# A bidirectional mLSTM and gated feed-forward block on eight cores: contiguous weight layouts, a split last group, and a second gate buffer, other engine and other banks in the last backward sweep

## What is computed

```
h = modulate(rmsnorm(x, norm1_g), sh1, sc1)
z = h @ w_in                       # q,k | v | o | u,v of the gating unit | merge gates | 16 gate columns
qk = silu(centred_conv(qk, conv_w, conv_b))
hA = mlstm_bidirectional(qh, kh, vh, gates)        # forward scan + flipped backward scan, 4 heads x 256
y_a = rmsnorm_per_head(hA) * mh_g * sigmoid(o_a)
y_b = gelu(u_b) * (w_s applied to layernorm(gelu(v_b)) in chunks of 128 + b_s)
x = x + g1 * ((sigmoid(mg_a) * y_a + sigmoid(mg_b) * y_b) @ w_out)
h2 = modulate(rmsnorm(x, norm2_g), sh2, sc2)
x = x + g2 * (square(relu(h2 @ w1)) @ w2)
out = rmsnorm(x, normf_g)
```

## Time and profile before

| | us |
|---|---|
| median of 3 runs | 2370.88 |
| lowest, highest | 2370.76, 2378.68 |
| profiled execution | 2383.2 |
| span of its slowest core (core 1) | 2381.6 |
| span of its fastest core (core 2) | 2346.8 |

### The profile page before, as it was taken

The page is one execution under the profiler, slowest core; times in us unless marked ns, Lnnn a source line. Parts: engine busy times, 40 slices in busy tenths (PEclk is TensorE's granted clock), DMA queues, the critical chain, the costliest instruction groups (busy, mean ns, idle before and its releaser), DMA issues.

```text
span 2381.6 us, 49251 instructions; the slowest of 8 cores (2346.8 to 2381.6 us)
## 1 busy us (share of the span) xinstructions
PE 2219.5 (93%) x15036; PEld 1339.7 (56%) x15036; DVE 1403.2 (59%) x3065; ACT 1129.8 (47%) x2274; POOL 948.9 (40%) x1154
## 2 busy tenths in 40 slices
PE   5989999979899999999867999999999999999997
PEld 1444545446566555555523566666666666666664
DVE  2757787768788878878758733343333334333432
ACT  4644554378676666666535533333333333333332
POOL 1646666112377666656646612212222222212221
PEclk7999999999999999999979999999999999999998
DMA  9645454225866755645666620111111111111000
GB/s 303 175 92 143 124 139 125 76 37 81 84 82 84 133 96 96 146 87 100 113 158 189 201 84 30 48 54 54 54 50 50 54 54 54 54 54 54 30 17 36
DMA packets 141937, 219.96 MB, mean 92 GB/s; under 512 B 15655, under 2 KB 96103, under 8 KB 136686
## 3 DMA queue, kind: packets, MB, share of 16 engines
q1 hardware_dynamic: 104718, 187.16, 25.2%
q0 software_dynamic: 36960, 29.66, 13.4%
HBM read 196.08 MB, written 79.71 MB: 116 GB/s over the span
## 4 chain that ended last, share of the span: by engine, by line
PE 75%; DVE 8%; DMA 7%; issue 6%; POOL 2%; ACT 1%; DVEq 0%; SPq 0%; POOLq 0%; ACTq 0%
PE ps L359 73%; DVE arena L399 5%; PE ps L371 2%; DMA hf_d<-arena 2%; POOL arena L394 1%; ACT arena L379 1%; DMA arena<-w_vum 1%; DVE arena L394 1%; DMA mixa_d<-arena 1%; DMA arena<-x 1%; DMA mix_d<-arena 1%; DMA arena<-wg_d 1%; DMA arena<-hf_d 1%; DMA w_d<-w 0%; DVE arena L391 0%
## 5 line engine op out<-in xcount | busy, mean ns | idle before, releaser
L359 PE MATMUL ps<-arena 128*128 128x512 bf16 (+7 forms) x14012 | 2176.9, 321 | 129.5 <-DVE arena L399 46.9
L359 PEld LDWEIGHTS ps<-arena 128*128 128x128 bf16 (+1 forms) x14012 | 1279.3, 98 | 986.7 <-issue 227.8
L394 POOL TENSOR_TENSOR arena<-arena 128x1 f32<-128x1 f32 (+3 forms) x648 | 697.5, 1084 | 1057.6 <-ACT arena L379 352.9
L399 DVE SCALAR_TENSOR_TENSOR arena<-ps,arena 128x256 bf16<-128x256 f32 (+6 forms) x1474 | 606.1, 414 | 635.0 <-ACT arena L379 489.4
L379 ACT ACTIVATE arena<-ps 128x256 f32<-128x256 f32 (+2 forms) x972 | 496.7, 524 | 848.5 <-PE ps L359 719.3
L379 ACT ACTIVATE arena<-arena 128x514 bf16<-128x514 f32 (+5 forms) x558 | 403.7, 733 | 266.0 <-DVE arena L399 98.3
L399 DVE SCALAR_TENSOR_TENSOR arena<-arena 128x256 bf16<-128x256 f32 (+3 forms) x257 | 271.6, 1057 | 63.8 <-POOL arena L394 24.4
L379 ACT ACTIVATE arena<-ps,arena 128x512 f32<-128x512 f32 (+3 forms) x512 | 252.9, 519 | 117.2 <-DVE arena L1049 31.6
L394 DVE TENSOR_TENSOR arena<-ps,arena 128x512 bf16<-128x512 f32 (+4 forms) x294 | 169.2, 583 | 104.4 <-PE ps L359 102.2
L391 POOL TENSOR_SCALAR arena<-arena 128x1 f32<-128x1 f32 (+2 forms) x317 | 152.1, 482 | 149.4 <-ACT arena L379 121.2
L399 DVE SCALAR_TENSOR_TENSOR arena<-arena,ps 128x514 f32<-128x514 f32 x240 | 178.7, 745 | 28.4 <-PE ps L359 25.0
(11 more groups left out here) (17 smaller groups left out, 86.8 us busy)
## 6 DMA issues: line engine op xcount, KB each, us to landing
arena<-x SPq DMA_DIRECT2D x64, 512.0 KB, 4.6
arena<-w_ada SPq DMA_DIRECT2D x8, 2048.0 KB, 10.2
hf_d<-arena SPq DMA_DIRECT2D x128, 128.0 KB, 4.1
arena<-hf_d SPq DMA_DIRECT2D x128, 128.0 KB, 3.3
w_d<-w POOLq DMA_DIRECT2D x32, 512.0 KB, 8.6
out<-arena SPq DMA_DIRECT2D x32, 512.0 KB, 3.2
arena<-w_d SPq DMA_DIRECT2D x13, 1024.0 KB, 5.9
arena<-w_vum SPq DMA_DIRECT2D x12, 1024.0 KB, 16.9
```

The lines of the kernel that those rows point to most:

```text
L359: ins = e.matmul(o_, l_, r_, start=st, stop=sp)
L394: return E(eng, lambda e, o_=o_, a_=a_, b_=b_, op=op: e.tensor_tensor(o_, a_, b_, op), reads, writes, 0.6 if op == ALU.pow else vcost(eng, ...
L399: e.scalar_tensor_tensor(o_, a_, sc, b_, op0, op1), reads, writes, vcost("dve", o_))
```

## The change

1. The host packs w_qkv, w_og, w_out, w1 and w2 so that each casting transfer reads one contiguous run and writes one; the number and bytes of the transfers stay.
2. In the head x tiles 2 and 3 are asked for after w_vum piece 3.
3. Of the extra buffers, gv[2] moves to the second half of wad[5], and vn[2..4] all lie in wad[7].
4. For head 3 the gate weights have a buffer of their own (wog2, at base_b, where wqkv was), loaded once the last block is prepared (nxt == 31) instead of at hF = 4; wog is then free for feed-forward weights.
5. In the last sweep the sigmoid's scaling is an activation Copy on ACT instead of an operation on DVE, and the backward numerator alternates between banks 4 and 5.
6. In the last group the last three ffn2 steps are done for the first 128 rows and then for the second, each followed by final_last: as final, but in halves of 512 columns, straight from the banks, with DVE doing the second half's sums.

```diff
@@ head and stage 2
-            if n in (1, 3, 4):
-                load_x({1: 2, 3: 3, 4: 4}[n])
+            if n == 3:
+                load_x(2)
+                load_x(3)
+            if n == 4:
+                load_x(4)
...
-                dst, c0, rr = wq_d[h][j][:, 2 * m:2 * m + 2, :], (0, 1024, 2048)[j] + h * 256, R("wq_d", h, j, m)
+                ps_ = slice(32 * m, 32 * m + 32)
+                dst, src, rr = wq_d[h][j][ps_].rearrange("p a b -> p (a b)"), w_qkv[h][j][ps_], R("wq_d", h, j, m)
...
-            DMA("pool", dst, w_in[m * 256:(m + 1) * 256, c0:c0 + 256].rearrange("(kc p) n -> p kc n", p=128), [], [rr], gs_, pace=after)
+            DMA("pool", dst, src, [], [rr], gs_, pace=after)
...
-        SCH.alias([("wad", 7)], [("gv", 2, 0), ("gv", 2, 1), ("vn", 2), ("vn", 3)])
+        SCH.alias([("wad", 7)], [("vn", 2), ("vn", 3), ("vn", 4)])
...
-        gv.append(xbuf[1][:, 0, :])
-        vx = xbuf[1][:, 1, :].bitcast(BF16)
-        vn += [vx[:, 0:1024], vx[:, 1024:2048], wad[5][:, 1024:1536].bitcast(BF16)]
+        gv.append(wad[5][:, 1024:2048])
+        vx = wad[7].bitcast(BF16)
+        vn += [vx[:, j * 1024:(j + 1) * 1024] for j in range(3)]
...
-        SCH.alias([("gu", 2, 0), ("gu", 2, 1), ("gu", 3, 0), ("gu", 3, 1), ("gv", 2, 0), ("gv", 2, 1), ("vn", 2), ("vn", 3)], [("wst",)])
+        SCH.alias([("gu", 2, 0), ("gu", 2, 1), ("gu", 3, 0), ("gu", 3, 1), ("vn", 2), ("vn", 3), ("vn", 4)], [("wst",)])
@@ mLSTM
+        def RW(h):
+            return R("wog2") if h == 3 else R("wog")
+
         def load_og(h):
-            DMA("sp", wog, wg_d[h], [R("wg_d", h, j, m) for j in range(2) for m in range(4)], [R("wog")], wog_sem)
+            if h == 3:
+                wogs.append(alloc([128, 8, 512], BF16, ["wog2"], at=base_b))
+            DMA("sp", wogs[h // 3], wg_d[h], [R("wg_d", h, j, m) for j in range(2) for m in range(4)], [RW(h)], wog_sem[h // 3])
...
+        def BNB(h, i):
+            return (4, 5)[i % 2] if h == 3 else 5
...
-                TS("dve" if hF is None else "pool", tg[k2], tg[k2], 0.5, 0.5, ALU.mult, ALU.add, [RT], [RT])
+                if hF is None:
+                    ACTF(tg[k2], tg[k2], AF.Copy, [RT], [RT], scale=0.5, bias=0.5)
+                else:
+                    TS("pool", tg[k2], tg[k2], 0.5, 0.5, ALU.mult, ALU.add, [RT], [RT])
...
-                casts.append((w1_d[j][:, 4 * m:4 * m + 4], w1[m * 512:(m + 1) * 512, j * 512:(j + 1) * 512].rearrange("(kc p) n -> p kc n", p=128), R("w1_d", j, m)))
+                casts.append((w1_d[j][64 * m:64 * m + 64].rearrange("p a b -> p (a b)"), w1[j][64 * m:64 * m + 64], R("w1_d", j, m)))
...
-            if 1 < hF:
+            if 1 < hF < 4:
                 load_og(hF - 1)
...
+                if nxt == 31:
+                    load_og(3)
@@ feed-forward
+        def final_last(g, s_):
...
+            for hh, cs in enumerate(hv):
+                TT("dve", tf[s_][:, cs], banks[4 + 2 * s_ + hh][:, :], g2s[:, cs], ALU.mult, [PB(4 + 2 * s_ + hh), R("g2s")], [R("tf", s_, hh)])
+                TT("dve" if s_ else "pool", X[:, cs], tf[s_][:, cs], X[:, cs], ALU.add, [R("tf", s_, hh), R("xg", kg, s_)], [R("xl", s_, hh)])
+                ACTF(tf[s_][:, cs], X[:, cs], AF.Square, [R("xl", s_, hh)], [R("tf", s_, hh), R("s5", so, hh)],
+                     accum_out=sm4[:, so + 3 + hh:so + 4 + hh])
...
+            for hh, cs in enumerate(hv):
+                STT(tf[s_][:, cs], X[:, cs], sm4[:, so + 5:so + 6], nfs[:, cs], ALU.mult, ALU.mult,
+                    [R("xl", s_, hh), R("r5", so), R("nfs")], [R("tf", s_, hh)])
+                out_ops.append(DMA("sp", out[i * 128:(i + 1) * 128, cs], tf[s_][:, cs], [R("tf", s_, hh)], [R("out", i, hh)], (ob_sem, mxi_sem)[hh][s_]))
...
-                ffn2(g, ft)
+                if nx is not None or ft < 29:
+                    ffn2(g, ft)
+                elif ft == 31:
+                    for s_ in range(2):
+                        for f_ in (29, 30, 31):
+                            ffn2(g, f_, (s_,))
+                        final_last(g, s_)
```

More of the change, by code:

```diff
@@ L262, in build_program @@
     w_gt = din("w_gt", [128, 128])
+    w_qkv = din("w_qkv", [4, 3, 128, 2048])
+    w_og = din("w_og", [4, 128, 4096])
     bifb = din("bifb", [128, 512])
@@ L845, in build_program @@
         sml = alloc([128, NSM * 8], F32, [(nm, m) for nm in ("sml", "sq") for m in range(NSM)])
-        wog = alloc([128, 8, 512], BF16, ["wog"])
-        wog_sem = new_dsem()
+        wogs = [alloc([128, 8, 512], BF16, ["wog"])]
+        wog_sem = [new_dsem() for _ in range(2)]
         for s_ in range(1, NS):
@@ L1034, in chunk_pair @@
             if aF is None:
-                den, wvn, n_ = banks[BN["B"]][:, 256:257], wvi[:, aB:aB + 1], 1
-                rb = [PB(BN["B"])]
+                den, wvn, n_ = banks[BNB(hB, iB)][:, 256:257], wvi[:, aB:aB + 1], 1
+                rb = [PB(BNB(hB, iB))]
                 dn, rd = sml[:, so + 1:so + 2], sml[:, so + 3:so + 4]
@@ L1054, in chunk_pair @@
             if hB is not None:
-                STT(hs[k2], banks[BN["B"]][:, 0:256], sml[:, so + 3:so + 4], hfi[k3], ALU.mult, ALU.add,
-                    [PB(BN["B"]), RSM, R("hfi", k3)], [R("hs", k2)])
+                bn = 5 if hF is not None else BNB(hB, iB)
+                STT(hs[k2], banks[bn][:, 0:256], sml[:, so + 3:so + 4], hfi[k3], ALU.mult, ALU.add,
+                    [PB(bn), RSM, R("hfi", k3)], [R("hs", k2)])
                 RS2 = R("sq", t % NSM)
@@ L1106, in build_program @@
         now = {("wqkv", p_) for p_ in range(3)} | {("kT", k, j) for k in range(2) for j in range(2)} | {("acc", k) for k in range(3)}
+        now |= {("wog",)}
         now |= {("v", "F", k, j) for k in range(2) for j in range(2)} | {("P", "F", k) for k in range(2)}
@@ L1111, in build_program @@
         freed(now, 0)
+        freed({("wog2",)}, 9)
         for k in range(8):
@@ L1244, in ffn1, with ffn2 @@
             STT(fT[b4], banks[bk][:, 0:256], 0.0, sq4[c3], ALU.is_gt, ALU.mult, [PB(bk), R("sq4", c3)], [R("fT", b4)])
-        def ffn2(g, ft):
+        def ffn2(g, ft, ss_=(0, 1)):
             bk = ft % 4
-            for s_ in range(2):
+            for s_ in ss_:
                 for hh in range(2):
@@ L1276, in final @@
                 out_ops.append(DMA("sp", out[ts_, :], tf[s_], rt, [R("out", i)], ob_sem[s_]))
+        def final_last(g, s_):
+            kg = g % 2
+            i = 2 * g + s_
+            so = (i % 32) * 8
+            X = xg[kg][s_]
+            hv = [slice(hh * 512, (hh + 1) * 512) for hh in range(2)]
+            for hh, cs in enumerate(hv):
[3 more added lines that the diff above has]
+                     accum_out=sm4[:, so + 3 + hh:so + 4 + hh])
+            TS("dve", sm4[:, so + 6:so + 7], sm4[:, so + 3:so + 4], sm4[:, so + 4:so + 5], 1.0 / D, ALU.add, ALU.mult,
+               [R("s5", so, 0), R("s5", so, 1)], [R("v5", so)])
+            TS("dve", sm4[:, so + 6:so + 7], sm4[:, so + 6:so + 7], EPS, None, ALU.add, None, [R("v5", so)], [R("v5", so)])
+            RSTD(sm4[:, so + 6:so + 7], sm4[:, so + 5:so + 6], R("v5", so), R("r5", so))
+            for hh, cs in enumerate(hv):
+                STT(tf[s_][:, cs], X[:, cs], sm4[:, so + 5:so + 6], nfs[:, cs], ALU.mult, ALU.mult,
+                    [R("xl", s_, hh), R("r5", so), R("nfs")], [R("tf", s_, hh)])
+                out_ops.append(DMA("sp", out[i * 128:(i + 1) * 128, cs], tf[s_][:, cs], [R("tf", s_, hh)], [R("out", i, hh)], (ob_sem, mxi_sem)[hh][s_]))
         g0 = order_g[0]
@@ L1334, in build_program @@
                     fn()
-            evac(g)
-        final(order_g[-1])
+            if nx is not None:
+                evac(g)
         return finish(nc, SCH, esem, out_ops)
@@ L1416, in host_inputs @@
         "bsp": np.ascontiguousarray(np.asarray(b_s[0], f).T),
-        "w_out": np.ascontiguousarray(w_out[0], dtype=f),
-        "w1": np.ascontiguousarray(w1[0], dtype=f),
-        "w2": np.ascontiguousarray(w2[0], dtype=f),
+        "w_qkv": np.stack([np.stack([kp(w_in[0][:, c0 + h * 256:c0 + h * 256 + 256]) for c0 in (0, 1024, 2048)]) for h in range(4)]),
+        "w_og": np.stack([kp(np.concatenate([w_in[0][:, c0 + h * 256:c0 + h * 256 + 256] for c0 in (3072, 6144)], axis=1)) for h in range(4)]),
+        "w_out": np.stack([kp(w_out[0][:, j * 512:(j + 1) * 512]) for j in range(2)]),
+        "w1": np.stack([kp(w1[0][:, j * 512:(j + 1) * 512]) for j in range(8)]),
+        "w2": np.stack([kp(w2[0][j * 512:(j + 1) * 512]) for j in range(8)]),
         "nfgb": bc(normf_g),
```

22 lines of the change are left out of this document (11 added, 11 removed).

## The result

| | before | changed |
|---|---|---|
| median us (6 runs each, same chip) | 2373.03 | 2359.23 |
| ratio, with its 95% interval | | 0.9938 [0.9923, 0.9952] |
| profiled execution | 2383.2 | 2360.78 |
| spans of the cores in it | 2346.8 to 2381.6 | 2346.2 to 2359.2 |

What follows compares the result with a forecast made beforehand. PE was taken as the bound in the feed-forward, with gains only in its idle time elsewhere. Terms 6 + 8 + 9 + 10 + 5.5 = 38.5 us gave 2332.4 from the median 2370.9; it took 2336, range 2310 to 2359.

Steps and rivals of the forecast that it cites:

- Head, 6: In the head, tile 3's store goes ahead of the w_ada load: 6.0 us gained, bounds 0 and 6.6.
- Casts, 8: Contiguous weight casts relieve the DMA engines before 830 us: 8 us gained, bounds minus 3 and 20.
- what POOL spends on issuing stays: Step in the casts' term: POOL's time for issuing the 116 weight casts doesn't change; no size given.
- Gate weights, 9: Before the last sweep, wg3 in its own buffer loads 40 us earlier: 9 us gained, bounds 0 and 20.
- the traffic stays the bound: Rival: same bytes, small stores still wait, gate and sweep terms fall to 2; about 2347 us, chance 0.20.
- I take 9 of the 13.1 us idle: Gate weights' step, 1209 to 1227 us: 9 of PE's idle time won, plus 3 before, less 3 for added wait.
- The last sweep, 10: Last backward sweep, 1227 to 1361 us: scaling moved to ScalarE, two banks; 10 us gained, bounds minus 5 and 25.
- 20.9 us taken off VectorE's busy time would come off PE's wait: Last sweep's step: 32 scalings leave VectorE, for which PE waits 14.7 us before 128x257 matmuls; 10 us taken.
- Tail, 5.5: After PE's last matmul, work in halves cuts 15.8 us to 10.3: 5.5 us gained, bounds 4 and 7.
- Long casts block the queue: Rival: 36 long cast pieces each hold all engines 3.2 us, delaying small transfers; about 2455 us, chance 0.03.
- The gains don't add: Rival: each removed wait uncovers another, only tail and head's store gains remain; about 2359 us, chance 0.06.
- The prediction's own test: Wrong in its core if the 861 us from 500 us to the feed-forward's start shrink by less than 15 us.

Runs made afterwards that it cites:

- p_tail: The kernel before with the new tail alone (last three steps' matmuls by halves, final_last behind each): 2371.81 us, ratio 0.9990.
- p_head: The kernel before with the head's swapped buffers and reordered x loads alone: 2367.02 us, ratio 0.9972.
- a_early: The changed kernel with the 36 late casts (w_out, w1, w2) back in the old layout: 2358.74 us, ratio 0.9924.
- best: The changed kernel with the last sweep's output product put after the next chunk's state update, and an added DRAIN on POOL in the last feed-forward group: 2347.68 us, ratio 0.9873.
- p_casts: The kernel before with the casts' new contiguous layout alone: 2365.03 us, ratio 0.9961.

## Why the prediction was wrong where it was

- **Head, 6.** Right: 6.7 us alone. But the casts remove the same wait, so in the whole one of the two gains nothing here. The sum counted the store's wait for the head, and half of the other idle time for the casts, and never asked whether the casts caused that wait. (The casts' upper bound, half of the idle time from 60 to 1166 but for that wait, is 23.5 us by the rows, not 20.)
- **Casts, 8.** Alone 9.3 us faster by the ratio and 5.4 by the mean span, in spite of 4.8 us more tail, so the relief, 10 to 14 us, is larger than the term. About 6.4 of it is the head's wait; the rest, 3.6 to 5.2 us of the stretch (1837.5 against p_tail's 1841.1 and p_head's 1842.7), is what the casts add in the whole. It lies in the early casts, as said (a_early). The Trainium skill's 512 B for line rate (DMA: Bandwidth & Descriptors, Specifications) would have made this term 0. The written packets of the earlier trace rows, 482 bytes in the mean, lie a little under that figure, so no run here tests the figure itself; the runs do speak against counting packets so near to it as free, since longer packets of the same bytes gave the 9.3 us. The step "what POOL spends on issuing stays" failed: the casts leave POOL's DRAIN 6.4 us longer at the program's end, which nothing in the prediction looked at, and they shorten POOL's issuing, by 9 us for the 48 casts of q, k and v.
- **Gate weights, 9.** Measured -1 to 2. wg3 was issued at 1151.58, 58 us earlier than before (40 forecast), and still nothing came of it. The rival "the traffic stays the bound" had this right: the stores and the state load wait in wg3's place. The step that failed is "I take 9 of the 13.1 us idle": idle time beside a transfer was credited to that transfer, while the queue behind it held as much.
- **The last sweep, 10.** The sign was wrong: the move of the scaling cost 3.5 to 7.4 us, the second bank gave 0.8 to 4.2. The step that failed is that 20.9 us taken off VectorE's busy time would come off PE's wait. VectorE's list is in order: with the scaling moved it stood 8.9 us instead of 4.6 in front of the output product, until POOL had the norm's power, with the state update behind. The prediction asked what stands behind ScalarE's added instructions on the way to PE, and not what VectorE itself waits for. That a lighter VectorE is worth about 10 us was right, but only with the output product moved, which the change doesn't do: the stretch is 1827.0 in best and 1837.5 in p_casts, which has none of the sweep's edits (the gate weights' -1 to 2 us are in this difference).
- **Tail, 5.5.** The new tail is worth 3.3 to 3.4 us, below the lower bound of 4: VectorE ends its products and sums 3.8 us behind PE, not 2.6, and the end of the span comes 4.2 us behind the last issue, not 3.7. In the changed kernel the DRAIN hides all of it.
- **The rivals.** "Long casts block the queue" didn't come: PE works 271 us of 280 in 500 to 780, where it worked 265. "The gains don't add" came nearest in time (2359) by another road: two parts on one wait, one part behind a cost of another, and one with the wrong sign.
- **The prediction's own test** was that it is wrong in its core if the stretch from 500 us to the feed-forward's start shrinks by less than 15 us. On core 1 it shrank by 19 (1361 to 1342), and yet the forecast failed: 8.5 of the 19 come from ahead of the first state store (507.7 to 499.2), and before's profile was of a long execution.
- The summed terms, each as measured in the whole: head and casts together 8.0 ahead of the first store, 4 in the stretch, gates -1 to 2, the scaling -3.5 to -7.4, the second bank 0.8 to 4.2, tail 0: 4 to 15 us. The mean span fell by 11.8. That the median is that of the rival "the gains don't add" is luck, since the road was another.

## What to carry to other kernels

Before work is moved to a less busy engine, look at what the engine that gets lighter will wait for, through the queues that get longer, and at what stands behind that wait in its own order; move the waiting operation back first, then the work. Two edits can be worth much more together than one by one, as the second bank and the order here: test them together as well. When two edits each remove the same wait, count it once. Look at what ends last at the program's end, the engines' closing instructions too, since a gain ahead of it is lost behind it.
